# A head's second exponential ahead of an eviction, and GpSimd's finishing work in two column ranges, in the second attention of a two-block transformer kernel

## The reference

```python
outs = []
for start in range(0, L, Q_BLOCK):                    # blocks of 128 queries
    end = start + Q_BLOCK
    qb = q[:, start:end]; kb = k[:, :end]; vb = v[:, :end]
    s = jnp.einsum('bqhd,bkhd->bhqk', qb, kb).astype(jnp.float32) * scale
    mask = jnp.arange(start, end)[:, None] >= jnp.arange(end)[None, :]
    s = jnp.where(mask[None, None], s, -jnp.inf)
    p = jax.nn.softmax(s, axis=-1).astype(vb.dtype)
    outs.append(jnp.einsum('bhqk,bkhd->bqhd', p, vb))
o = jnp.concatenate(outs, axis=1).reshape(B, L, N_HEADS * V_HEAD_DIM)
return o @ w_o
```

## Time and profile before

| | us |
|---|---|
| Median of 3 runs | 2121.5 |
| Lowest and highest run | 2120.63, 2122.65 |
| The profiled execution | 2121.44 |
| Its span in the profile | 2119.7 |
| The second attention in it | about 1029 to 1195 |
| PE busy over the span | 2023.6 (95%) |

### The profile page before, as it was taken

One profiled execution on the slowest core, in us unless ns is written; L12 is line 12 of the kernel. 1 busy time (PEld: TensorE's weight loads), 2 busy tenths in 40 slices (PEclk: granted clock), 3 DMA queues, 4 the chain that ended last, 5 costly groups with the idle time before them and its releaser, 6 DMA issues.

```text
span 2119.7 us, 35722 instructions
## 1 busy us (share of the span) xinstructions
PE 2023.6 (95%) x13506; PEld 1826.6 (86%) x13506; DVE 873.1 (41%) x1601; ACT 835.6 (39%) x1347; POOL 836.6 (39%) x508
## 2 busy tenths in 40 slices
PE   8999999998999999989888899999999989999997
PEld 6888888887777778979766789999999879999997
DVE  6873531037543330257456364334400573334103
ACT  3223433325543442245455444344323454344331
POOL 1545424432434444234444334433344134443441
PEclk7999999998999999989999999999999999999999
DMA  9642002221322233222100012222232112322331
GB/s 359 248 169 80 16 17 98 95 74 40 107 81 99 97 102 100 71 71 90 50 1 1 25 56 86 93 89 79 89 104 96 41 50 80 99 92 86 109 101 41
DMA packets 54957, 184.47 MB, mean 87 GB/s; under 512 B 6992, under 2 KB 10320, under 8 KB 54864
## 3 DMA queue, kind: packets, MB, share of 16 engines
q1 hardware_dynamic: 53024, 180.97, 25.1%
q10 hardware_dynamic: 1840, 2.19, 0.3%
HBM read 181.03 MB, written 2.10 MB: 86 GB/s over the span
## 4 chain that ended last, share of the span: by engine, by line
PE 87%; DVE 7%; issue 2%; ACT 2%; POOL 1%; DMA 1%; DVEq 0%; ACTq 0%; SPq 0%; POOLq 0%
PE PS L742 70%; PE PS L1031 2%; PE PS L859 2%; PE PS L938 2%; PE PS L907 1%; DVE work L2820 1%; PE PS L823 1%; PE PS L985 1%; DVE ada_acc L2364 1%; PE PS L1290 1%; PE PS L850 1%; PE PS L1111 1%; PE PS L1099 1%; PE PS L1447 1%; ACT work L1963 1%
## 5 line engine op out<-in xcount | busy, mean ns | idle before, releaser
L1496 POOL TENSOR_TENSOR w_lo<-w_raw,w_hi 128x1024 fp32r<-128x1024 f32 x263 | 638.0, 2433 | 934.0 <-ACT w_hi L1666 933.9
L742 PE MATMUL PS<-H_hi,w_lo 128*128 128x256 f32 (+3 forms) x2088 | 561.8, 320 | 20.6 <-DVE H_lo L2767 8.0
L1666 ACT ACTIVATE w_hi<-w_raw 128x1024 fp32r<-128x1024 f32 (+2 forms) x307 | 295.3, 981 | 717.8 <-PE PS L742 664.6
L742 PE MATMUL PS<-H_lo,w_hi 128*128 128x256 f32 (+3 forms) x2088 | 554.6, 317 | 0.0
L742 PE MATMUL PS<-H_hi,w_hi 128*128 128x256 f32 (+3 forms) x2088 | 553.6, 316 | 0.0
L742 PEld LDWEIGHTS PS<-H_hi,w_lo 128*128 128x128 f32 x2088 | 351.9, 191 | 59.4 <-issue 13.6
L742 PEld LDWEIGHTS PS<-H_hi,w_hi 128*128 128x128 f32 x2088 | 352.4, 191 | 25.7
L742 PEld LDWEIGHTS PS<-H_lo,w_hi 128*128 128x128 f32 x2088 | 352.5, 191 | 24.5
L2820 DVE SCALAR_TENSOR_TENSOR work<-PS,vec,work 128x512 f32<-128x512 f32 (+4 forms) x264 | 187.0, 751 | 440.5 <-ACT work L1963 431.0
L742 PE MATMUL PS<-mid_hi,w_lo 128*128 128x256 f32 (+2 forms) x968 | 228.5, 294 | 3.6 <-DVE work L2820 3.6
L742 PE MATMUL PS<-mid_hi,w_hi 128*128 128x256 f32 (+2 forms) x968 | 226.9, 292 | 0.0
(11 more groups left out here) (364 smaller groups left out, 2840.4 us busy)
## 6 DMA issues: line engine op xcount, KB each, us to landing
w_raw<-stream SPq DMA_DIRECT2D x289, 512.0 KB, 3.2
ada_w<-ada SPq DMA_DIRECT2D x48, 512.0 KB, 6.7
X<-xT SPq DMA_DIRECT2D x8, 256.0 KB, 5.5
yT<-X SPq DMA_DIRECT2D x16, 128.0 KB, 1.7
rel_raw<-rel ACTq DMA_DIRECT2D x4, 256.0 KB, 2.8
vec<-vecs ACTq DMA_DIRECT2D x1, 390.0 KB, 4.1
sin_t<-rope ACTq DMA_DIRECT2D x1, 264.0 KB, 2.9
cos_t<-rope ACTq DMA_DIRECT2D x1, 132.0 KB, 2.4
```

The costliest lines, as they stand in the source:

```text
L742: last = pe.matmul(out[:, c0 + a:c0 + b], w, x[:, a:b], start=start and i == 0, stop=stop and i == 2)
L1496: gp.tensor_tensor(w_lo[:, o], w_raw[:, o], w_hi[:, o].bitcast(F32), ALU.subtract)\
L1666: return act_.activation(out, in_, ACT.Copy, scale=scale)
```

## The change

Two things are changed, both in `attention2`.

First, in ACT's `step`, `exps(p, t)` comes before the copy `weights(p, t - 1)` at pos 1. At all other places of the head the order of the two was empty.

Second, `finish_o2` works on columns 0 to 255 and 256 to 527 apart: four operations for a pair instead of two. The first half waits for the early part of par 1 (t = 3), the second for the late part (t = 6). In GpSimd's loop the first half stands ahead of `lower_qk2(p+1, 0)`, the second where the whole stood. `fin_ok` counts two for a pair and starts at 2; `take_out` waits for the half that covers its own columns, for the early part (t = 8) and now also for the late part (t = 1 of the next pair); `round_o` waits for both halves.

```diff
@@ GpSimd
             gp.sem_inc(w_lo_ok, RING)
+            gp.sem_inc(fin_ok, 2)
...
-            def finish_o2(p):
-                gp.wait_ge(o_ok, part2(p, 1, 1) + 2)
-                gp.wait_ge(o_hi, p + 1)
-                gp.tensor_tensor(half2, half2, twice2, ALU.mult).then_inc(two_ok, 1)
-                gp.wait_ge(two_ok, p + 1)
-                gp.tensor_tensor(O2[:, :], twice2, half2, ALU.subtract).then_inc(fin_ok, 1)
+            def finish_o2(p, late):
+                c = slice(256, S2) if late else slice(0, 256)
+                gp.wait_ge(o_ok, part2(p, 1, late) + 2)
+                if not late:
+                    gp.wait_ge(o_hi, p + 1)
+                gp.tensor_tensor(half2[:, c], half2[:, c], twice2[:, c], ALU.mult).then_inc(two_ok, 1)
+                gp.wait_ge(two_ok, p * 2 + (late + 1))
+                gp.tensor_tensor(O2[:, c], twice2[:, c], half2[:, c], ALU.subtract).then_inc(fin_ok, 1)
...
             with gp.Fori(1, H2 // 2 - 1) as p:
+                finish_o2(p - 1, 0)
                 lower_qk2(p + 1, 0)
-                finish_o2(p - 1)
+                finish_o2(p - 1, 1)
                 lower_qk2(p + 1, 1)
                 lower_o2(p - 1)
             for p in (H2 // 2 - 2, H2 // 2 - 1):
-                finish_o2(p)
+                finish_o2(p, 0)
+                finish_o2(p, 1)
                 lower_o2(p)
@@ ScalarE
                 def round_o(p):
-                    act_.wait_ge(fin_ok, p + 1)
+                    act_.wait_ge(fin_ok, p * 2 + 4)
...
                 def step(p, t, first, last):
                     par, pos = divmod(t, 5)
+                    exps(p, t)
                     if pos == 1:
                         weights(p, t - 1, first)
-                    exps(p, t)
@@ VectorE
-                def take_out(p, par, late, first=False):
+                def take_out(p, par, late):
                     v.wait_ge(inv_ok, part2(p, par, late))
-                    if not first and par + late == 0:
-                        v.wait_ge(fin_ok, p)
+                    if par == 0:
+                        v.wait_ge(fin_ok, p * 2 + (late + 1))
```

More of the change, by code:

```diff
@@ L2604, in step @@
                     if pos == 3 and not (first and par == 0):
-                        take_out(*before2(p, par), 0, first)
+                        take_out(*before2(p, par), 0)
                 maximum(0, 0)
```

## The result

| | before | after |
|---|---|---|
| Median, us | 2121.26 (4 runs) | 2091.79 (4 runs) |
| Lowest and highest run, us | 2120.63, 2122.65 | 2091.15, 2092.46 |
| Span of the profiled execution, us | 2119.7 | 2089.3 |
| Mean granted clock of PE | 0.978 | 0.982 |

The ratio of after to before is 0.986, with a 95% interval of 0.9843 to 0.9877. The median fell by 29.5 us, where 24.7 were forecast as the likeliest; the time lies in the stated range and 0.6 us from the case "all falls go" (2092.4), which had a chance of 0.25. That it lies there is in good part by accident, as will be seen: only one of the two falls at the edges went. Of seven further executions of the kernel before, on the chip of the experiments e1 to e4, one took 8123.37 us; it is left out of what follows.

A forecast was written before the change was run, and what follows sets the result against it. PE, busy 95%, bounds the kernel, with waits in the second attention from ACT's queue order and GpSimd's Newton step. Gains 13.7 + 8.3 + 2.7 (clock falls) = 24.7 us off 2121.44 give 2096.8 us; range 2091.0 to 2105.0.

The forecast's parts named there:

- all falls go: Rival, chance 0.25: PE's clock falls at the edges of the attention go too, 4.4 us more, 2092.4 us.
- the two falls at the edges: PE clock falls at 1032 to 1035 and 1189 to 1196, both left in the forecast as staying.
- The first part: Second attention, scores at pos 1: exponential ahead of ACT's copy removes PE's idle time in 16 heads, 13.7 us.
- signs of being wrong: Wait for ACT at scores of pos 2, late low parts of q and k, or clock falls costing more than now.
- The second part: Newton in halves shortens seven PE waits before products at pos 4: 1.38 to 0.23, last 2.63 to 1.26; 8.3 us.
- The room ahead of the low parts: GpSimd's low parts, queued behind the first half, end at least 1.7 us before PE's scores need them; cost 0.
- the first half holds up the next pair: Rival, chance 0.02: slow GpSimd half delays the low parts, PE waits, seven pairs lose 6 us; 2127 us.
- ACT's next: Third exponential ends at +0.94, fourth due about +1.84, ACT's tightest place: cost 0, at most 1.6 us in all.
- The clock: Three PE clock falls within the attention go because PE's busy share rises; 2.7 us more.
- The sum: Whole kernel: 13.7 + 8.3 + 2.7 = 24.7 us gained, 2096.8 us; chance 0.45.
- The rival of ports: Rival, chance 0.06: GpSimd's added operations and certain DVE operations take shared SBUF ports by turns; gain 12.7 us, 2108.7 us.

The follow-up runs named there:

- e1: First part alone: the kernel before with only ACT's second exponential ahead of its copy, Newton step whole; 2107.92 us, ratio to before 0.9929.
- e4: Kernel after, with DVE's eviction of the early part at pos 3 ahead of the copy and the next maximum; 2085.36 us, ratio to before 0.9829.
- e6: Kernel after, with five more GpSimd operations in the first Newton half, ahead of the low parts; 2109.59 us, ratio to before 0.9943.
- e2: Second part alone: kernel after with ACT's old order restored, Newton step in halves; 2109.16 us, ratio 0.9941.
- e5: Kernel after, with two more GpSimd operations in the first Newton half, ahead of the low parts; 2092.11 us, ratio to before 0.9866.
- e3: Kernel after, with the first Newton half behind the next pair's low parts, directly ahead of the second half; 2091.60 us, ratio 0.9862.
- e7: Kernel of e4, with DVE's eviction of the late part moved from the end of pos 1 to that of pos 2; 2090.82 us, ratio to before 0.9854.

## Why the prediction was right or wrong

**The first part: the mechanism right, the term too small.** All 16 waits at pos 1 went, with their 13.7 us of idle time, and ACT has the two operations in the new order. One new wait came: 0.53 us in the first head, at scores of pos 2 (1032.84), which is one of the signs of being wrong that I had named. They wait for the third tile's exponential, and ACT has there, in pair 0 alone, a rounding of k between the copy and that exponential (`k_hi`, 1031.54 to 1032.18). So the idle time gained is 13.2 us. The step that failed is another: I took a wait to cost what its idle time says: in pair 3, 0.94 and 0.82. The starts of the matmuls tell more. Before, the scores started 1.27 us behind the start of the transpose (1100.15 to 1101.42); after, 0.09 (1104.46 to 1104.55): 1.18 us. In the even head it is 1.07 by the same reckoning (1110.67 to 1111.82 before, 1096.19 to 1096.27 after). The idle time is counted from the modelled end of the transpose, 0.33 us behind its start, and a matmul that needn't wait starts ahead of that end. Each of these waits cost 0.25 us more than its row said, 0.49 in a pair. So the term of the waits was too small: a pair after the change took not 16.92 us but 16.48, 2.6 us over six pairs and about 1 us more in the first and the last. e1 shows it alone (17.64, where the idle times give 18.07), e6 shows it at a wait of another kind (2.28 us for 2.04), and e4 before products, where it is 0.15 us a wait.

**The second part: right.** The wait was worked out to go from 1.38 to 0.23, in the last pair from 2.63 to 1.26; measured are 0.23 and 1.30. e2 has it alone: 1.12 us a pair, with 1.15 forecast. A wait that is shortened and not removed gains just the difference of its idle times. GpSimd's operations on 256 columns took 0.73 us, just under my 0.75 to 0.92. The room ahead of the low parts was worked out as "at least 1.7 us" and was 1.8; e5 and e6 bracket it. The rival "the first half holds up the next pair" exists as a mechanism, from 1.8 us of more work on, and is far from this change.

**ACT's next: right.** The third tile's exponential ended 1.1 us behind the start of the scores (1105.65 to 1104.55) and the fourth started at +1.99, where I had +0.94 and +1.84 counted from a start 0.2 us later. In the loop no scores of pos 2 wait; the one that does, in pair 0, I had not looked at. The tightest place on ACT cost nothing that the trace shows.

**The clock: three falls gone as forecast, the reason for it not mine and still open.** I argued from a stretch that was busy 51.65 of 53 us, thus from the busy share. e1 and e2 tell that this is not what decides here: with 0.90 of the time busy there were four falls, with 0.86 none. Nor does the length of the single wait settle it. In the kernel before, only one of the three falls starts at a wait for GpSimd (1.37 us, at 1086.61). The two others start at the scores that waited for ACT, 0.94 and 0.95 us, ahead of GpSimd's wait in the same pair:

```profile
1141.11 0.41 PE L907 MATMUL PS<-k_hi,q_lo 128*72 128x256 f32 x1 [0.94 <-ACT work L1899]
...
1161.55 0.38 PE L907 MATMUL PS<-k_hi,q_lo 128*72 128x256 f32 x1 [0.95 <-ACT work L1899]
```

```profile
1136.00:1140.00 4.00, 3.73 (x22) 2.78 (x22) 2.70 (x7) 1.56 (x4) 1.69 (x2) 1.00 0.00 0
1140.00:1144.00 4.00, 3.06 (x13) 2.50 (x13) 1.23 (x3) 2.02 (x5) 0.00 (x0) 0.65 0.00 0
```

e2 keeps twelve waits of 0.82 to 0.95 us in its six pairs and has no fall there. e1, which has none of those, has its four falls at waits for GpSimd of 1.37 and 1.38 us, in four of six pairs, and e6 has four behind its six waits of 2.0 us. By kernel there is a line: the three whose loops have a wait of over 1 us in each pair (before, e1, e6) have falls in the loop, and the six whose longest wait there is 0.95 us or less (after, e2, e3, e4, e5, e7) have none. So the three falls went with the second part, and its worth is 8.3 + 2.7 us; that of the first is the waits. But a fall of the kernel before can stand at a wait of 0.94 us, and which waits bring one no run here settles. Alone the parts gave 14.3 and 13.0 us, 27.3 together against the 29.5 of both: e1 lost more to the clock than the kernel before.

**The edges.** I left both in. The first, at 1032 to 1035, starts within a wait of 0.73 us. It stands in the two kernels that have this wait (before and e2) and in none of the seven with ACT's new order. The first pair gave 2.34 us, where the waits of 0.73 at its two scores at pos 1 give 1.5; the fall is in the rest, less than 1 us. The last stayed, behind the 1.30 us of the last pair:

```profile
1160.00:1164.00 4.00, 3.45 (x13) 0.67 0.00 0
1164.00:1168.00 4.00, 4.00 (x19) 0.50 0.00 0
```

e4's 0.84 us there had no fall behind them. That is no proof that the shorter wait spared it, for e7 had none either, behind a wait as long as the kernel after's:

```profile
1160.44 0.89 PE L938 MATMUL PS<-PT,V 128*128 128x256 f32 x4 [1.27 <-DVE work L2593]
```

And both had a fall of 6.8 us in the output projection (from 1215 and from 1222), where the kernel after had one of 3.4 (from 1226), so a part came back.

**The sum.** Forecast 24.7: waits 13.7, Newton 8.3, falls 2.7. Found about 29.5: waits some 17.3 (13.2 of idle time and 16 x 0.25), Newton 8.2, the three falls 2.7, and the rest, 1 to 2 us, of the first fall and of changes outside the stage. The rival "all falls go" had the right time for another reason: it had 4.4 us from two falls where less than 1 us came from one, and nearly 4 us from the size of the waits. The rival of ports has nothing left: DVE's evictions took 0.43 and 0.42 us as before and its copies of 128x384 0.54. The exclusive turns of which the Trainium skill ("SBUF — State Buffer", section "SBUF: two separate sides") speaks show nowhere among these forms, of which none has both inputs in SBUF.

## What to carry to other kernels

Read the price of a wait of PE from the starts of the matmuls on both sides of it, beside a place where the same pair of matmuls runs without a wait: the idle time in the row leaves out the overlap that the wait destroys, here 0.25 us a wait behind a transpose, 0.15 before the products with v. An engine's queue order is the first thing to look at when a producer idles just before it makes what the bottleneck wants. Before moving an operation, list who waits for it on every engine, also two steps on: the same eviction moved ahead gave 6 us, and its sister moved back by one step took 5 away, through GpSimd and a rounding that nobody was looking at.

## What the runs showed of the hardware

The granted clock of PE fell from 2.4 to 1.2 GHz at single waits in a stream of matmuls, at some of them and not at others. The waits that a fall stood at were of 0.73, 0.94, 0.95, 1.3 to 1.4, 2.0 and 2.6 us; most waits of 0.7 to 1.4 us had none, 1.38 at 1107.96 in the kernel before and 1.27 in the last pair of e7 among them. In the loops, falls stood only in kernels with a wait of over 1 us in each pair, and not in one that was idle for more of the time: 115.88 us busy of 134 at clock 1.00 (e2), against 123.73 of 136 at 0.92 (e1). A fall lasted 3.4 or 6.8 us and cost some 1.5 or 3.0 where no wait absorbed it. By the Trainium skill ("TensorE: Matmul & The Clock Gate", part 1) idleness closes the gate; these rows agree in that every fall here in the attention starts in a wait or within 2.1 us behind one, and the share of idle time over the stage is no guide to it.
